# A hybrid trunk kernel: experts in 16 rounds instead of 18, and two more places for expert tiles beside a 4 KB descriptor scratch

## What is computed

```python
def hierarchical_moe(x, lp):
    ...
    g_logits = (xt @ lp['rg_w'] + lp['rg_b']).astype(jnp.float32)
    _, g_idx = lax.top_k(g_logits, 1)
    ...
    top_v, top_i = lax.top_k(e_logits, TOP_K)          # 2 of the 8 experts of the group
    weights = (p_grp * jax.nn.softmax(top_v, axis=-1)).astype(x.dtype)
    expert_idx = g_idx * EXPERTS_PER_GROUP + top_i
    y = grouped_expert_mlp(xt, expert_idx, weights, lp['e_wg'], lp['e_wu'], lp['e_wd'])

# for the rows xb of one expert e
    return (jax.nn.silu(xb @ wg[e]) * (xb @ wu[e])) @ wd[e]
```

## Time and profile before

| | |
|---|---|
| median of 3 runs | 1409.8 us (1404.47 to 1411.97) |
| profiled execution | 1408.7 us, span 1406.9 us |
| TensorE busy | 1218.9 us, 87% |
| VectorE busy | 722.8 us, 51% |
| DMA | 334.54 MB, mean 238 GB/s |
| granted clock of TensorE, mean | 0.941 |

### The profile page before, as it was taken

The page is one execution under the profiler, slowest core; times in us unless marked ns, Lnnn a source line. Parts: engine busy times, 40 slices in busy tenths (PEclk is TensorE's granted clock), DMA queues, the critical chain, the costliest instruction groups (busy, mean ns, idle before and its releaser), DMA issues.

```text
span 1406.9 us, 19405 instructions
## 1 busy us (share of the span) xinstructions
PE 1218.9 (87%) x7082; PEld 710.5 (50%) x7082; DVE 722.8 (51%) x1639; ACT 284.4 (20%) x708; POOL 112.9 (8%) x171
## 2 busy tenths in 40 slices
PE   5999999889886798999959999988989579898891
PEld 3455545554452565566424554556445356566560
DVE  3365877782476132332362687877643723332334
ACT  1211153750121000000022103357211110000000
POOL 2000000001001111111000000000100011111100
PEclk9999999999888999999989999999999779999996
DMA  9321101347149999999960201014562399999996
GB/s 375 150 94 50 54 17 61 129 177 308 41 177 401 416 418 418 418 418 417 410 252 31 90 33 60 1 68 181 198 252 104 138 398 418 417 418 417 419 415 250
DMA packets 61199, 334.54 MB, mean 238 GB/s; under 512 B 11856, under 2 KB 11856, under 8 KB 29100
## 3 DMA queue, kind: packets, MB, share of 16 engines
q1 hardware_dynamic: 45504, 295.78, 52.2%
q0 software_dynamic: 15600, 37.50, 7.0%
HBM read 322.41 MB, written 27.61 MB: 249 GB/s over the span
## 4 chain that ended last, share of the span: by engine, by line
PE 50%; DMA 27%; DVE 10%; issue 4%; ACT 3%; DVEq 2%; SPq 1%; PEld 1%; POOL 1%; PEldq 0%; ACTq 0%; POOLq 0%
DMA U<-in_stream 14%; PE bank L1748 12%; PE bank L1679 9%; PE bank L2160 8%; DMA ring<-in_stream 8%; PE bank L2193 6%; PE bank L2047 4%; DMA U<-in_n2row 3%; PE bank L1623 1%; DVE U L1267 1%; PE bank L1836 1%; DMA U<-moe_out 1%; PE bank L1862 1%; PE bank L2141 1%; SPq L382 1%
## 5 line engine op out<-in xcount | busy, mean ns | idle before, releaser
L2160 PE MATMUL bank<-U,HT 128*64 128x256 f32 (+2 forms) x1088 | 174.9, 400 | 24.2 <-DMA U<-in_stream 16.5
L1748 PE MATMUL bank<-HT,ring 128*128 128x512 f32 (+1 forms) x640 | 175.4, 435 | 2.0 <-issue 2.0
L1679 PE MATMUL bank<-ring,HT 128*128 128x512 f32 x320 | 147.0, 601 | 2.9 <-ACT HT L649 1.5
L2160 PEld LDWEIGHTS bank<-U,HT 128*64 128x64 f32 (+2 forms) x1088 | 117.8, 147 | 62.4 <-issue 40.1
L2160 PE MATMUL bank<-ring,HT 128*64 128x256 f32 (+2 forms) x736 | 132.4, 402 | 12.8 <-DMA ring<-in_stream 9.1
L1748 PEld LDWEIGHTS bank<-HT,ring 128*128 128x128 f32 x640 | 97.3, 191 | 79.7 <-issue 79.7
L1110 DVE SCALAR_TENSOR_TENSOR U<-U,prm 128x655 f32<-128x655 f32 x120 | 107.9, 899 | 8.0 <-issue 0.8
L2160 PEld LDWEIGHTS bank<-ring,HT 128*64 128x64 f32 (+2 forms) x736 | 86.4, 154 | 46.2 <-issue 28.6
L2047 PE MATMUL bank<-ring,HT 128*128 128x512 f32 x240 | 106.6, 594 | 0.0
L1541 DVE TENSOR_TENSOR HT<-bank,HT 128x256 f32<-128x256 f32 x36 | 15.3, 424 | 174.4 <-ACT HT L879 174.4
L2193 PE MATMUL bank<-U,HT 128*64 128x512 f32 (+2 forms) x288 | 90.8, 596 | 9.5 <-DMA U<-in_stream 6.0
(11 more groups left out here) (363 smaller groups left out, 1652.2 us busy)
## 6 DMA issues: line engine op xcount, KB each, us to landing
ring<-in_stream SPq DMA_DIRECT2D x138, 1024.0 KB, 7.3
U<-in_stream SPq DMA_DIRECT2D x96, 1024.0 KB, 22.7
RAB<-in_stream SPq DMA_DIRECT2D x16, 1024.0 KB
U<-moe_out SPq DMA_DIRECT2D x20, 512.0 KB, 7.4
U<-in_stream SPq DMA_DIRECT2D x16, 512.0 KB
CAT<-in_stream SPq DMA_DIRECT2D x16, 512.0 KB
RAB<-mod_rows POOLq DMA_DIRECT2D x12, 512.0 KB, 8.8
moe_in<-CAT POOLq DMA_DIRECT2D x10, 512.0 KB, 3.3
```

The lines of the kernel that those rows point to most:

```text
L1679: ins = e.matmul(bank[:], HT[:, k, t * P:(t + 1) * P], wide(q, k), start=(k == 0), stop=(k == KD - 1))
L1748: ins = e.matmul(out, wt(q)[:, k, P * (n % 2):P * (n % 2) + P], HT[:, k, lo:lo + w], start=(k == 0), stop=(k == KD - 1))
L2160: ins = e.matmul(PS[2 + p][s, FF * j:FF * j + FF], xgT[:, p, k, s], w, start=(k == 0), stop=(k == KD - 1))
```

## The change

1. `BIGS` and `MIDS` go from 8 and 16 to 7 and 14, and the rounds from 18 to 16. A fixed expert now has 96 slots, and a ranked expert of 32 slots sits beside it in the same round. Its gate, up and down products are cut into pieces of 64, 32 and 32 columns (`sides`). The slot arithmetic on VectorE gets five small operations.
2. Two more places, `spare`, in a buffer of their own. They take the first two tiles of the fixed experts, ahead of the wait for `u_free`. The space comes from a smaller scratch for the descriptors of GpSimd's transfers (4096 bytes of each partition), from `diag` moved into `U`, and from smaller constants (`ones`, `ones16`, `iota`).
3. Several semaphores are merged into one (`gated` and `cat_rdy` to `chunk_rdy`, `xd_rdy` and `w_rdy` to `scaled_rdy`, four to `chosen`), since two more places need four semaphores.

```diff
-FIXED, BIGS, MIDS, SMALLS = 3, 8, 16, 8
+FIXED, BIGS, MIDS, SMALLS = 3, 7, 14, 8
+BESIDE = BIGS + MIDS + SMALLS
-ROUNDS = list("PPFPFQBPBPPFBQBBPP")
+ROUNDS = list("PPFPFQBPFBPBQBPP")
-RING, EXT, LATE_TILES = 6, 5, 3
+RING, SPARE, INU, LATE_TILES = 6, 2, 5, 3
+EXT = SPARE + INU
...
-    blocks = {"F": [(n, (n,)) for n in range(FIXED)],
+    blocks = {"F": [(n, (n, BESIDE + n)) for n in range(FIXED)],
...
-    return sorted(tiles_used(), key=lambda tile: ROUNDS[tile[0]] != "F")
+    return sorted(tiles_used(), key=lambda tile: blocks[tile[0]][1][tile[2]] >= FIXED)
...
+        spare = sb("spare", [P, SPARE, SLOT])
-        ones = sb("ones", [P, P])
+        ones = sb("ones", [P, 1])
-        diag = sb("diag", [P, 4, P])
+        diag = view(2 * NLT * 256, 4, P)
...
+                for i in range(SPARE):
+                    load_expert(i)
                 e.wait_ge(S["u_free"], l + 1)
-                for i in range(EXT):
+                for i in range(SPARE, EXT):
                     load_expert(i)
...
-                e.tensor_scalar(small(1660, NE), rank, float(BIGS), 2.0, ALU.min, ALU.mult); dr()
+                e.tensor_scalar(small(1660, NE), rank, float(BIGS), 2.0, ALU.min, ALU.mult)
+                e.tensor_scalar(apart, rank, float(FIXED), float(-QUART), ALU.is_lt, ALU.mult)
+                e.tensor_scalar(beside, rank, 3.0, float(3 - 4 * BESIDE - 3 * BIGS - MIDS), ALU.mult, ALU.add); dr()
                 e.tensor_tensor(capm, capm, step, ALU.add)
-                e.tensor_tensor(at0, at0, small(1660, NE), ALU.add); dr()
+                e.tensor_tensor(at0, at0, small(1660, NE), ALU.add)
+                e.scalar_tensor_tensor(out=beside, in0=rank, scalar=float(BESIDE), in1=beside, op0=ALU.is_ge, op1=ALU.mult); dr()
+                e.tensor_tensor(capm, capm, apart, ALU.add)
+                e.tensor_tensor(at0, at0, beside, ALU.add); dr()
...
-                    n = P // len(blocks[r][1])
-                    return [(a, slice(n * a, n * a + n)) for a in range(P // n)]
+                    n, lanes_of = blocks[r]
+                    if n < FIXED:
+                        q = 64 * (n % 2)
+                        return [(0, slice(q, q + 64), False), (0, slice(64 - q, 96 - q), True), (1, slice(96 - q, P - q), True)]
+                    w = P // len(lanes_of)
+                    return [(a, slice(w * a, w * a + w), True) for a in range(P // w)]
...
-    nc = _bacc.Bacc("TRN2", target_bir_lowering=False, num_devices=1)
+    nc = _bacc.Bacc("TRN2", target_bir_lowering=False, num_devices=1, dynamic_dma_scratch_size=4096)
```

More of the change, by code:

```diff
@@ L69, in round_blocks @@
 def round_blocks():
-    blocks = {"F": [(n, (n,)) for n in range(FIXED)],
-              "B": [(n, (n,)) for n in range(FIXED, BIGS)],
-              "P": [(BIGS + n, tuple(BIGS + 2 * n + (a + n) % 2 for a in range(2))) for n in range(MIDS // 2)],
-              "Q": [(BIGS + MIDS // 2 + n, tuple(BIGS + MIDS + 4 * n + (a + 2 * n) % 4 for a in range(4))) for n in range(SMALLS // 4)]}
+    blocks = {"F": [(n, (n, BESIDE + n)) for n in range(FIXED)],
+              "B": [(n, (n,)) for n in range(FIXED, BIGS)]}
+    for kind, first, lane, w in (("P", BIGS, BIGS, 2), ("Q", BIGS + MIDS // 2, BIGS + MIDS, 4)):
+        count = (MIDS if w == 2 else SMALLS) // w
+        blocks[kind] = [(n, tuple(lane + w * (n - first) + (a + n % 2 * w // 2) % w for a in range(w)))
+                        for n in range(first, first + count)]
     return [blocks[kind].pop(0) for kind in ROUNDS]
@@ L266, in build @@
         nrow2 = view(LATER + 4 * D, D)
[L267 to L274, removed]
+        tabs = sb("tabs", [P, 2 * NBLK + 1 + NOVF + 3], I32)
+        slots, gidx = tabs[:, 0:NBLK], tabs[:, NBLK:2 * NBLK]
+        ovn = tabs[:, 2 * NBLK:2 * NBLK + 1 + NOVF]
+        lanes, gcur, scur = (tabs[:, 2 * NBLK + 1 + NOVF + j:2 * NBLK + 2 + NOVF + j] for j in range(3))
+        rows = sb("rows", [P, 4 * NT])
+        rowno = rows[:, 0:2 * NT].rearrange("p (k t) -> p k t", k=2)
+        rowhi = rows[:, 2 * NT:4 * NT]
         wov_gu = view(LATER, 2, KD, FF)
@@ L1413, in _ @@
                 e.tensor_reduce(rank, over, AX, ALU.add); dr()
+                apart, beside = small(1280, NE), small(1320, NE)
                 e.tensor_scalar(capm, rank, float(BIGS), float(HALF), ALU.is_lt, ALU.mult)
@@ L1766, in _ @@
                 e.matmul(PS[5][:, 40:80], triB[:], small(1060, 40), start=True, stop=True)
-                e.matmul(PS[5][:, 80:160], ones[:], small(1020, 80), start=True, stop=True).then_inc(S["cum_ps"], 1)
+                e.matmul(PS[5][:, 80:160], ones[:].to_broadcast((P, P)), small(1020, 80), start=True, stop=True).then_inc(S["cum_ps"], 1)
                 for n in range(4, 10):
@@ L2153, in up @@
                             e.wait_ge(S["hh_rdy"], m - 1)
-                    for a, s in both:
+                    for a, s, whole in both:
                         arrived((l, r, j, a))
                     for k in range(KD):
-                        for a, s in both:
+                        for a, s, whole in both:
                             key = (l, r, j, a)
@@ L2161, in up @@
                                            start=(k == 0), stop=(k == KD - 1))
[L2162 removed]
+                            if k == 0 and s == both[-1][1]:
                                 settle(ins)
[L2164 to L2165 removed]
+                            if k == KD - 1 and whole:
+                                if j and s == both[-1][1]:
                                     ins.then_inc(S["gu_ps"], 1)
```

92 lines of the change are left out of this document (46 added, 46 removed).

## The result

The changed kernel takes 1417.32 us (median of 6 runs, 1416.01 to 1422.43) against 1410.1 us for the kernel before in the same session (6 runs, 1404.47 to 1412.26). The ratio is 1.0064, with a 95% interval of 1.0038 to 1.0089: **slower by 0.64%**, where 1407 was forecast and the range ended at 1414. The profiled execution took 1417.72 us, with a span of 1416.0.

What follows compares the result with a forecast made beforehand. The prediction took saturated DMA in the expert stages as the bound, with TensorE having about 25 us of room. 1408.7 - 5.0 - 0.7 + 2.4 + 1.3 = 1406.7, rounded to 1407 us; range 1399 to 1414.

Steps and rivals of the forecast that it cites:

- The step that failed: TensorE's fixed rounds: column groups run side by side, so the uneven cut costs at most 2.9 us more, gate and up.
- A 64 | 32 | 32 round runs its groups one after another: Rival on TensorE's fixed rounds: +15 us in each, 240 us of work per layer, 1407 to 1415 us; chance 0.03.
- The two tiles fewer, -5.0 us: Layer 0's expert stage: two fixed tiles already in spare leave two fewer to move after 445 us, 2 x 2.5 us saved.
- The hole in layer 1, -0.7 us: Start of layer 1's expert stage: two more ring tiles fill a dip in the transfers at 1132 to 1134 us, saving 0.7 us.
- The small writes, +1.2 us for each layer: GpSimd's mod_rows writes before u_free: the early tiles delay them by 1.2 us per layer, bounds 0 and 3, +2.4 us together.
- the small writes wait for the whole backlog: Rival: GpSimd's small writes land only once the queued tiles are through, 3 us for each layer, 1410.3 us; chance 0.12.
- The slot arithmetic, +0.65 us for each layer: VectorE's table chain: five small operations and one more dependent level cost 0.65 us per layer, +1.3 us together.
- Sixteen rounds at 0 us: Expert stages: two fewer rounds save TensorE time, but all of it lies beside the DMA and goes into waiting, 0 us.
- TensorE's relief counts: Rival in the expert stages: less TensorE work shortens them, to 1360 to 1375 us in full or 1395 to 1401 partly; chance 0.14.
- The scratch at nothing: GpSimd's row loads behind u_free: the 4 KB scratch costs nothing; the rival, 7 us per layer and 1421 us, had chance 0.08.

Runs made afterwards that it cites:

- e1_even: The changed kernel with a fixed round cut into four pieces of 32 columns instead of 64, 32 and 32: 1410.3 us against 1408.46 for the kernel before.
- e2_wide_first: The changed kernel with all steps of the 64-column piece first, then those of the two 32-column pieces: 1411.67 us against 1408.46 for the kernel before.
- e3_places_only: The changed kernel with the 18 rounds and slot arithmetic of before, keeping the two places, early tiles and small scratch: 1408.74 us against 1408.46 before.
- e5_even_early: The changed kernel with four pieces of 32 columns and the two early tiles issued ahead of the output projection's tiles: 1403.88 us against 1408.7 before.
- e9_before_rows: The kernel before, with SyncE waiting for the landing of GpSimd's five row loads instead of for u_free: 1394.41 us against 1407.48.
- e10_places_early_rows: The kernel before (18 rounds) plus the two places, early tiles ahead of the output projection and SyncE's wait for the row loads: 1387.43 us against 1407.48.
- e6_scratch_only: The kernel before with the 4 KB scratch and nothing else: 1409.23 us against 1408.7, ratio 1.0001.
- e4_rounds_only: The changed kernel with four pieces of 32 columns, without the two places, early tiles and small scratch: 1409.7 us against 1408.46 for the kernel before.
- e8_even_early_rows: The changed kernel with 32-column pieces, early tiles ahead of the output projection, and SyncE waiting for GpSimd's row loads: 1386.81 us against 1408.7 before.

## Why the prediction was wrong

**The step that failed** is in the part on sixteen rounds: "So column groups run side by side, and a fixed round cut 64 | 32 | 32 costs per step between 0.23 and 0.32 us: at most 16 x 2 x 0.09 = 2.9 us more for its gate and up tiles." The rows under it show equal widths only, pairs of 64 and fours of 32. For 64 beside 32 there was no row, and I took the rule of equal widths over without a bound for its failure. Measured: 1.13 us per step of two passes, that is 0.57 per pass against my 0.23 to 0.32, and +15.1 us per fixed round. The widths take turns: 0.22 us for a pass of 64, 0.22 for a pair of 32, and 0.13 for each change of width. The upper end, 0.32, was misread too: the fours of 32 in the earlier trace rows run through a drop of the granted clock from 1.00 to 0.50 at about 532 us, and at a clock of 1.00 they take 0.22 each, as e1_even shows. The windows of the kernel before:

```profile
530.80:531.30 0.50, 0.50 (x12) 0.38 (x16) 0.00 (x0) 0.00 (x0) 0.00 (x0) 1.00 1.03 434
532.30:532.80 0.50, 0.50 (x12) 0.34 (x8) 0.00 (x0) 0.00 (x0) 0.00 (x0) 0.50 1.08 443
```

Undoing the uneven cut alone (e1_even) brings the median from 1417.3 to 1410.3 and the DMA share back to 1.01.

**The rival that named it** ("A 64 | 32 | 32 round runs its groups one after another") had the kind of failure right and was given 0.03. Its numbers fit in part by luck. It priced three passes in a row for gate and up, 32 x 0.46 = 15 us, and nothing for the down part, where the same working gives 7 more. Measured are 10.7 for gate and up and 4.5 for down, since the two sides of 32 do run side by side and the turns cost extra; the sum happens to be 15. The busy time of 240 us was then met as well (240.25 and 236.98). Its time, 1407 to 1415, was too low because I judged it by the mean: 240 of 250 us just fits. But a fixed round brings TensorE 26 us of matmuls for six tiles, which are 15 us of transfers, so the load comes in bursts, and the places in store carry a burst only in part (172 GB/s in 540 to 545 us). The changed kernel loses 11.4 us in its stages although neither is full on average. How many tiles in store a burst would need was not measured; e2_wide_first only shows that 21.5 us per round is hidden and 26.0 not. The loss by medians, 7 to 8 us from e1_even, is smaller than these 11.4 us of single profiles; the intervals are too wide to say by how much.

**The two tiles fewer, -5.0 us:** right. The stage of layer 0 is 5.6 to 6.2 us shorter in e1_even, e3_places_only and e5_even_early, and that of layer 1 as long as before. Between e9_before_rows and e10_places_early_rows it is only 2.7 us (259.4 against 256.7). In the changed kernel it was eaten by the fixed rounds.

**The hole in layer 1, -0.7 us:** not to be seen. Those three kernels have 249.6, 249.6 and 249.9 us against 249.7; but e6_scratch_only and e9_before_rows, which have no extra places either, have 251.4 and 251.2, so 0.7 us is below what single profiles can tell.

**The small writes, +1.2 us for each layer:** right mechanism, mis-sized: a delay of the read-back of 3.5 and 3.8 us, three times the term. They took 5.0 and 5.3 us to land instead of 1.7, and the read-back came 3.5 us late in layer 0 and 3.8 in layer 1 (7.0 behind the first write instead of 3.2), beyond my upper bound of 3. Of layer 0's delay 1.55 us reached the rank counts (425.03 against 423.48), while that of layer 1 reached the gather whole (125.0 against 120.5 us behind the writes, with 0.65 for the slots). That is 5.35 us where the sum has +2.4. What e5_even_early shows is that the same writes, with the tiles moved away, are back at 1.48 us, and 6 us of the median with them. The rival "the small writes wait for the whole backlog", at 3 us for each layer, was the better forecast of this term, and the windows of the changed kernel fit it: the transfers are full until 322 us, and the writes have landed by 323.72, when the read-back starts. That a write waits for all of the backlog was not tested by itself.

**The slot arithmetic, +0.65 us for each layer:** measured 0.65 in layer 0 (the terms written out add up to 0.67).

**Sixteen rounds at 0 us:** right for even sides (e4_rounds_only, and e8_even_early_rows beside e10_places_early_rows). This also settles the rival "TensorE's relief counts", which had 1395 to 1401 us: 13 to 15 us less TensorE time in a stage buys nothing beyond the interval of some 3 us. The forecast had some 20 us less; the granted clock, 0.92 and 0.93 where it was 0.96, took a part.

**The scratch at nothing:** right (e6_scratch_only). GpSimd's row loads are 0.53 us long and follow each other at once, but for one gap of 0.29 us behind the first; e4_rounds_only, with the usual scratch, has 0.28 us there.

The sum with the measured terms, for the changed kernel: 1408.7 - 5.6 (tiles) + 11.4 (uneven rounds) + 1.3 (slots) + 1.55 (writes, layer 0) + 3.8 (writes, layer 1) gives 1421. The span came out at 9.1 us more, 3 below this; the stretch between the stages was 2.8 us shorter in this profile than in that of before, at a granted clock of 0.98 against 0.92 in its last 85 us. No run ties that part to the change.

## What to carry to other kernels

Before column groups of different widths are put into one step, take a row that shows just that mix: equal widths run side by side, unequal ones queued here and paid for each turn, and four pieces of the narrowest width cost nothing extra even though there are more of them. Judge an engine's room by the stretch with the densest work, not by the stage's mean. Check that the rows from which a price is read ran at the same granted clock. And where a small transfer stands on the path, look at what another queue issues ahead of it or with it: holding back a bulk load that nobody is waiting for was worth 1.0% by itself here, where the change as it stood cost 0.6%.

## What the runs showed of the hardware

- Passes of 256 columns in float32 with 64-wide and 32-wide weights don't overlap on TensorE: 9.05 us for a half in turn, 7.17 us grouped by width, 3.6 us as four times 32. One turn between widths costs 0.13 us.
- An 8 KB write of GpSimd's queue takes 1.7 to 1.9 us with no tile ahead of it and 5.0 to 5.3 us behind two tiles of 1 MB that SyncE issued 8 us earlier.
- A 512 KB row load of GpSimd's queue, the last of five, lands in 8.1 us with the stream held back (e9_before_rows) and in 22.1 us beside it (before), in layer 0.
- The same work ahead of layer 1's small writes takes 300.8 us where the granted clock stays at 1.00 in its last 85 us, and 307.6 us where it is 0.90 on the mean.
- 4 KB of scratch for descriptors serve this kernel's GpSimd transfers as well as the usual size: ratio 1.0001 [0.9978, 1.0024].
